# Mixer A: softmax denominators of eight key tiles by 128x32 products with ones in the four column groups of the array

## The chip, the cores and the metric

The kernel runs as one program on all 8 cores of one Trainium2 chip. Each core has its own TensorE (matrix products), VectorE, ScalarE, GpSimd, SyncE and DMA queues. Core c works on batch element c // 2 and on one half of its tokens as queries; cores don't exchange data. The metric is the time in microseconds of the slowest core. The profile pages and the rows below are of core 5, the slowest core of one profiled execution.

## The reference

One bidirectional encoder layer on x (4, 2048, 2048). What matters here is mixer A, a dense attention with 8 query heads and 2 key/value heads of width 128:

```python
h = rms_norm(x, norm_gain[l])
proj = jnp.einsum('bsd,dc->bsc', h, w_in[l])
...
qa = axial_rotary(rms_norm(qa.reshape(B, S, A_Q_HEADS, HEAD_DIM), q_norm_gain[l]), row_id, col_id)
ka = axial_rotary(rms_norm(ka.reshape(B, S, A_KV_HEADS, HEAD_DIM), k_norm_gain[l]), row_id, col_id)
ya = grid_gqa_attention(qa, ka, va) * jax.nn.silu(ga)       # (B, S, A_WIDTH)
```

with, inside the attention:

```python
s = jnp.einsum('bqhgd,bkhd->bhgqk', q_blk, k).astype(jnp.float32) * scale
p = jax.nn.softmax(s, axis=-1).astype(v.dtype)
return jnp.einsum('bhgqk,bkhd->bqhgd', p, v)
```

Mixer B (dilated windows in three groups), the merge of the two branches under sigmoid gates, the output projection with the residual and a final RMS norm follow.

## The kernel before

**Stages.** Each core first normalises its batch element's 2048 tokens into hT (2048 features by 2048 tokens, bfloat16). It then projects keys and values of mixer A, and after that runs two things interleaved on TensorE: the attention of mixer A, and the projections of mixer A's queries and gates and, as they finish, those of mixer B. Mixer B's attention comes next, again among projections, then the merge over 16 column tiles, then the output projection.

**One block of mixer A** is one head h and one half qb of the core's 1024 queries, 16 blocks in all. The 2048 keys are 16 tiles kc of 128. For each tile, attA_S makes the scores, transposed (128 keys by 512 queries), in one of three PSUM banks; ScalarE takes the exponential into one of eight buffers pbufs (0 to 3 in s_arena, 4 to 7 in s_gain), in bfloat16. No maximum is subtracted. attA_PV multiplies the tile with V and sums over the 16 tiles in bank 6.

**The denominators** are the column sums of P over all 2048 keys. A product with a 128x128 matrix of ones gives the sum over the 128 keys of a tile, in all 128 partitions at once. That is done directly for the tiles kc 3, 7, 11, 14 and 15, in bank 7. The other eleven tiles, DSET, are summed element by element on VectorE into acc (float32, in s_gain). Then acc is split into two bfloat16 parts, hiP (a cast) and loP (acc less hiP, a subtraction), and two more products with ones in bank 7 (in epi) add the sums of the two. ScalarE makes the reciprocal as exp(-ln), into rec, VectorE multiplies bank 6 with it (tmp) and then with the gate, into yaT.

**A P buffer** is free again when its product with ones was issued, or, for a tile of DSET, when both the V product and the add have read it (p_used counts to 2).

**Order of the work.** The program is written out ahead of time by a planner. Each of the generators (attA_S, attA_PV, attA_sum, epi, proj_all and others) yields after a small piece of work; Streams.run always emits the piece whose first operation could start soonest by the planner's own clock, less a small bonus of its stream. The clock (Sched.ready and Sched.cost) adds up a cost for every operation and 0.18 us for a result from another engine. Pools stand for banks and buffers: X.alloc takes an item or blocks the stream, X.free gives it back at that point of the program. The engines then run their own lists in that order, and wait on semaphores for each other.

**Banks.** While mixer A's attention runs, three banks (0, 1, 2) are the pool "pj" of the projections, three (3, 4, 5) the pool "S" of the scores, 6 is "Oa" and 7 is "La". A projection unit (16 products of 512 columns, in pieces of four) needs two free banks of pj and takes one; the sums of squares for the norm of q take one for a moment. Each block goes with two projection units, one of a query head and one of a gate head. pj_bonus keeps the projections at most a little ahead of the attention.

Bank 6 is held from the block's first V product until tmp has been made, so the next block's V products wait for the end of this one's denominators.

Of the kernel before, what the change touches and what calls it, by code (L numbers as in the profile page):

```python
# [8 lines left out]
BF16 = mybir.dt.bfloat16  # L9
AF = mybir.ActivationFunctionType  # L10
# [12 lines left out]
class Sched:  # L23
# [41 lines left out]
    def cost(self, eng, method, kw):  # L65
        out = kw["ap"] if "ap" in kw else kw["out"]
        n = 1
        for d in out.shape[1:]:
            n *= d
        if eng == "pe":  # L70
            return max(0.066, n / 2400.0 + 0.002)
        if eng == "act":
            return 0.17 + 0.00084 * n
        if eng == "dve":
            fast = "in0" in kw and kw["in0"].dtype == BF16 and out.dtype == BF16
            return 0.15 + n / (1920.0 if fast else 960.0)
        return 0.3 + n / 960.0
# [271 lines left out]
def build_nc(debug=False, stop_after=None):  # L349
# [24 lines left out]
    with es:  # L374
        es.enter_context(nc.allow_low_precision("bf16 matmul operands, fp32 accumulation"))

        def sb(name, shape, dt):
            return es.enter_context(nc.sbuf_tensor(name, shape, dt))
# [15 lines left out]
        one_t = sb("s_one_t", [128, 1], F32)  # L394
        stat = sb("s_stat", [128, 64], F32)
        ones_t = sb("s_ones", [128, 128], BF16)
        pb = [es.enter_context(nc.psum_tensor("pb%d" % i, [128, 512], F32)) for i in range(8)]
        S = Sched(nc, es)

# [12 lines left out]
        def PS(i):  # L412
            return ("ps", i)
# [12 lines left out]
        def MM(out, lhsT, rhs, start, stop, reads, writes, inc=None):  # L426
            S.op("pe", "matmul", dict(out=out, lhsT=lhsT, rhs=rhs, start=start, stop=stop), reads, writes,
                 inc=(stop if inc is None else inc))
# [4 lines left out]
        def ACT(out, in_, func, reads, writes, **kw):  # L433
            S.op("act", "activation", dict(out=out, in_=in_, func=func, **kw), reads, writes)
# [4 lines left out]
        def CP(out, in_, reads, writes, eng="dve"):  # L439
            S.op(eng, "tensor_copy", dict(out=out, in_=in_), reads, writes)  # L440
# [8 lines left out]
        def MEMSET(ap, val, writes, eng="pool"):  # L449
            S.op(eng, "memset", dict(ap=ap, constant=val), (), writes)  # L450
# [110 lines left out]
        MEMSET(ones_t[:], 1.0, ["ones"], eng="dve")  # L561
        MEMSET(eps_t[:], EPS, ["eps"], eng="dve")
        MEMSET(one_t[:], 1.0, ["one"], eng="dve")
        ACT(stat[:, 0:1], one_t[:], AF.Ln, ["one"], ["pre"])
        S.dma("pool", rsm[:], ropeA_d, "c_rsm", writes=["rsm"])
        S.dma("pool", gnt[:], gn_d, "c_gnt", writes=["gnt"])
# [89 lines left out]
        acc = gain[:, 1024:1536]  # L656
        hiP = gain[:, 1536:1792].bitcast(BF16)
        loP = gain[:, 1792:2048].bitcast(BF16)
        DSET = (0, 1, 2, 4, 5, 6, 8, 9, 10, 12, 13)
        rec = af(11776, 12288)  # L660
        tmp = af(12288, 12800)

# [230 lines left out]
            X.later(f)  # L893

        def attA_sum():
            for h in range(8):
                for qb in range(2):
                    yield from X.alloc("acc")
                    first = None
                    for kc in DSET:  # L900
                        yield from ge(("P", h, qb, kc), 1)
                        p = X.get(("P", h, qb, kc)) - 1
                        if first is None:
                            first = (p, kc)
                            continue
                        if first != 0:
                            TT(acc, pbufs[first[0]], pbufs[p], ALU.add, [("pbuf", first[0]), ("pbuf", p)], ["acc"])
                            p_used((h, qb, first[1]), first[0])
                            first = 0
                        else:  # L910
                            TT(acc, acc, pbufs[p], ALU.add, ["acc", ("pbuf", p)], ["acc"])
                        p_used((h, qb, kc), p)
                        yield
                    CP(hiP, acc, ["acc"], ["hiP"])
                    yield
                    TT(loP, acc, hiP, ALU.subtract, ["acc", "hiP"], ["loP"])
                    X.setf(("hl", h, qb))
                    yield

        def attA_PV():  # L920
            yield from ge("Oready", 1)
            for h in range(8):
                vtok = vatoks[h // 4]
                for qb in range(2):
                    yield from X.alloc("Oa")
                    pe_first = True
                    for kc in range(16):
                        yield from ge(("v", kc // 4, (kc // 2) % 2), 1)
                        yield from ge(("P", h, qb, kc), 1)
                        p = X.get(("P", h, qb, kc)) - 1  # L930
                        if kc not in DSET and pe_first:
                            yield from X.alloc("La")
                        MM(pb[6][:], vtok[:, kc * 128:(kc + 1) * 128], pbufs[p], (kc == 0), (kc == 15),
                           [("vatok", kc // 4, (kc // 2) % 2), ("pbuf", p)], [PS(6)], inc=(kc in DSET or kc == 15))
                        if kc not in DSET:
                            MM(pb[7][:], ones_bf, pbufs[p], pe_first, False, ["ones", ("pbuf", p)], [PS(7)], inc=True)
                            pe_first = False
                            X.free("pb", p)
                        else:
                            p_used((h, qb, kc), p)  # L940
                        X.later(partial(at_add, 1.0 / 32))
                        yield

                    def epi(h=h, qb=qb):
                        yield from X.alloc("ep")
                        yield from ge(("hl", h, qb), 1)
                        MM(pb[7][:], ones_bf, hiP, False, False, ["ones", "hiP"], [PS(7)], inc=True)
                        yield
                        MM(pb[7][:], ones_bf, loP, False, True, ["ones", "loP"], [PS(7)])
                        X.free("acc", 0)  # L950
                        yield
                        ACT(rec, pb[7][:], AF.Ln, [PS(7)], ["rec"])
                        X.free("La", 7)
                        yield
                        ACT(rec, rec, AF.Exp, ["rec"], ["rec"], scale=-1.0)
                        yield
                        TT(tmp, pb[6][:], rec, ALU.mult, [PS(6), "rec"], ["tmp"])
                        X.free("Oa", 6)
                        yield
                        yield from ge(("sg", h, qb), 1)  # L960
                        TT(yaT[:, h, qb * 512:(qb + 1) * 512], tmp, sgas[h % 2][:, qb * 512:(qb + 1) * 512], ALU.mult,
                           ["tmp", ("sga", h % 2, qb)], [("yaT", h)])
                        X.free("ep", 0)
                        X.bump("E_done")
                        yield
                    fork(epi(), 0.5, "epiA")
                    yield

# [626 lines left out]
```

How the kernel before makes its waits and increments, by code:

```python
            def body(engine, prog=prog):  # L239
                for fn, waits, inc in prog:
                    for (s, v) in waits:
                        engine.wait_ge(s, v)
                    if fn is not None:
                        ins = getattr(engine, fn[0])(**fn[1])
                        if inc is not None:
                            ins.then_inc(inc[0], inc[1])
```

## Time and profile before

| | |
|---|---|
| median of 3 runs | 1170.87 us (1170.75 to 1171.92) |
| profiled execution, its own time | 1173.17 us |
| span of its slowest core, from the first to the last instruction | 1171.5 us |
| spans of the 8 cores | 1163.4 to 1171.5 us |
| granted TensorE clock, mean of a core | 0.991 to 0.997 of full speed |
| busy: TensorE, VectorE, ScalarE | 1131.8 us (97%), 625.4 us (53%), 518.3 us (44%) |
| instructions of the span | 18014 |

The difference between the profiled execution's time and the span is what lies before the first and behind the last instruction. Almost all operations go through one helper, so that every row has line 244: rows are told apart by the names of the tensors (output <- inputs; pb is PSUM, numbers left out) and by their shapes (in a product, 128*128 is the part of the array that is used, and 128x512 the output). A product's busy time counts overlap once; products overlap, as each lasts longer than the time to the next start.

### The profile page before, as it was taken

What the parts mean: (1) busy time and instruction counts of PE and PEld (TensorE: products, weight loads), DVE (VectorE), ACT (ScalarE), POOL (GpSimd) and SP (SyncE); (2) the same over time, 40 slices, a digit from 0 to 9 for tenths busy, and PEclk for the clock granted to TensorE, in tenths of its full rate; (3) what the DMA queues carried; (4) which work ended last, traced back from release to release, by engine and by line L of the source; (5) the groups of instructions that cost most, each with busy time, mean ns of one, the idle gap of its engine ahead of it and who ended that gap; (6) DMA issues with size and microseconds to landing.
All of it is one profiled execution on the core that took longest, in us unless ns stands there. A gap on an engine that the chain in (4) does not pass through costs nothing.

```text
span 1171.5 us, 18014 instructions; the slowest of 8 cores (1163.4 to 1171.5 us)
## 1 busy us (share of the span) xinstructions
PE 1131.8 (97%) x6052; PEld 563.5 (48%) x6052; DVE 625.4 (53%) x980; ACT 518.3 (44%) x914; POOL 81.1 (7%) x166
## 2 busy tenths in 40 slices
PE   3799999999999999999999999999999999999996
PEld 1668444444444545554554454444444444444443
DVE  4779878888886655663655555521212122122155
ACT  4675688888886544543543544411111111111232
POOL 1000100000000000000000000011111111010000
PEclk9999999999999999999999999999999999999999
DMA  7982711222232423423432420155656645449533
GB/s 186 251 262 37 126 35 22 36 37 37 37 73 37 90 37 57 70 42 51 71 55 37 73 46 5 19 90 94 117 88 115 100 71 87 74 89 246 130 145 144
DMA packets 28761, 100.16 MB, mean 86 GB/s; under 512 B 3168, under 2 KB 7280, under 8 KB 25600
## 3 DMA queue, kind: packets, MB, share of 16 engines
q0 software_dynamic: 20400, 63.34, 32.8%
q1 hardware_dynamic: 8272, 35.67, 9.1%
q8 instruction: 51, 0.84, 0.3%
q14 instruction: 38, 0.31, 0.1%
HBM read 153.87 MB, written 8.39 MB: 139 GB/s over the span
## 4 chain that ended last, share of the span: by engine, by line
PE 91%; DMA 5%; DVE 1%; ACT 1%; issue 1%; ACTq 0%; DVEq 0%; POOLq 0%; SPq 0%
PE pb L244 91%; DMA s_wsl<-w_in 2%; DVE s_gain L244 1%; DMA s_ybT<-xt 1%; DMA s_hT<-xt 1%; DMA s_yaT<-xt 1%; DMA s_arena<-xt 1%; ACT s_arena L244 0%; DVE s_arena L244 0%; ACT s_gain L244 0%; DVE s_yaT L244 0%; ACT s_wsl L244 0%; ACT s_stat L244 0%; ACTq L1482 0%; DVEq L242 0%
## 5 line engine op out<-in xcount | busy, mean ns | idle before, releaser
L244 PE MATMUL pb<-s_hT,s_wsl 128*128 128x512 bf16 (+2 forms) x3584 | 749.3, 362 | 3.2 <-DVE s_hT L244 1.9
L244 PEld LDWEIGHTS pb<-s_hT,s_wsl 128*128 128x128 bf16 x3584 | 341.8, 98 | 361.0 <-issue 10.2
L244 ACT ACTIVATE s_arena<-pb 128x512 bf16<-128x512 f32 (+6 forms) x472 | 262.5, 573 | 248.6 <-PE pb L244 184.2
L244 DVE TENSOR_TENSOR s_arena<-pb,s_arena 128x512 f32<-128x512 f32 x112 | 89.2, 797 | 291.2 <-PE pb L244 284.9
L244 ACT ACTIVATE s_arena<-pb,s_mb 128x512 f32<-128x512 f32 x64 | 43.8, 687 | 246.2 <-PE pb L244 246.2
L244 PE MATMUL pb<-s_arena 128*128 128x512 bf16 (+3 forms) x704 | 138.2, 308 | 0.0
L244 DVE TENSOR_TENSOR s_arena<-s_arena 64x512 bf16<-64x512 f32 (+2 forms) x128 | 100.6, 786 | 19.8 <-ACT s_arena L244 12.5
L244 POOL DMA_DIRECT2D s_wsl<-w_in x92 | 48.9, 532 | 842.4 <-PE pb L244 762.2
L244 DVE TENSOR_TENSOR s_arena<-s_arena,s_rope 128x512 f32<-128x512 f32 (+3 forms) x136 | 89.8, 661 | 3.8
L244 PEld LDWEIGHTS pb<-s_arena 128*128 128x128 bf16 x704 | 60.1, 98 | 54.3 <-issue 2.8
L244 DVE TENSOR_TENSOR s_gain<-s_gain 128x512 f32<-128x512 f32 x96 | 66.3, 691 | 19.5 <-ACT s_gain L244 9.6
L244 ACT ACTIVATE s_gain<-pb 128x512 bf16<-128x512 f32 x128 | 69.6, 597 | 11.1 <-PE pb L244 9.9
L244 DVE TENSOR_TENSOR s_arena<-pb,s_rope 64x512 f32<-64x512 f32 (+1 forms) x64 | 40.7, 636 | 37.8 <-ACT s_arena L244 37.7
L244 PE MATMUL pb<-s_yaT,s_wsl 128*128 128x512 bf16 x256 | 57.9, 379 | 0.0
L244 PE MATMUL pb<-s_hT,s_arena 128*128 128x512 bf16 x256 | 55.4, 379 | 0.0
L244 ACT ACTIVATE s_arena<-s_arena 128x512 f32<-128x512 f32 x80 | 49.9, 631 | 11.5 <-DVE s_arena L244 7.8
L244 DVE TENSOR_TENSOR s_gain<-s_gain,s_arena 128x512 f32<-128x512 f32 x64 | 44.3, 692 | 10.6 <-DVE s_gain L244 9.5
L244 PE MATMUL pb<-s_gain,s_arena 128*128 128x512 bf16 x128 | 45.7, 383 | 0.1
L244 PE MATMUL pb<-s_wsl,s_ones 128*128 128x256 bf16 x128 | 18.5, 295 | 22.6 <-ACT s_wsl L244 22.6
L244 DVE COPY s_arena<-pb 128x1024 bf16<-128x1024 bf16 (+3 forms) x40 | 24.6, 615 | 29.0 <-PE pb L244 28.6
L244 PEld LDWEIGHTS pb<-s_yaT,s_wsl 128*128 128x128 bf16 x256 | 25.1, 98 | 30.2
L244 PEld LDWEIGHTS pb<-s_hT,s_arena 128*128 128x128 bf16 x256 | 25.0, 98 | 30.2
(77 smaller groups left out, 643.8 us busy)
## 6 DMA issues: line engine op xcount, KB each, us to landing
s_wsl<-w_in POOLq DMA_DIRECT2D x92, 512.0 KB, 5.1
y<-s_arena SPq DMA_DIRECT2D x14, 512.0 KB, 3.0
s_yaT<-xt SPq DMA_DIRECT2D x6, 1024.0 KB, 9.8
s_arena<-xt SPq DMA_DIRECT2D x4, 1024.0 KB, 17.3
s_wsl<-wba POOLq DMA_DIRECT2D x16, 256.0 KB, 4.0
s_hT<-xr SPq DMA_DIRECT2D x4, 1024.0 KB, 16.0
s_hT<-wout POOLq DMA_DIRECT2D x8, 512.0 KB, 33.4
s_ybT<-xt SPq DMA_DIRECT2D x2, 1024.0 KB, 16.1
```

The lines of the kernel that those rows point to most:

```text
L244: ins = getattr(engine, fn[0])(**fn[1])
```

## The change

Before, five tiles of a block go through full products with ones and eleven are summed on VectorE. After:

- VectorE sums seven tiles (0, 3, 6, 9, 12, 13, 14).
- Eight tiles form two quads, (1, 2, 4, 5) and (7, 8, 10, 11). When the V product of a quad's last tile has been issued, four products follow, one for each tile, with a 128x32 matrix whose elements are 1/32. The one of tile j of the quad writes the partitions 32j to 32j+31 of bank 7; the second quad adds to the first. Each partition of group j then holds 1/32 of the sum over the keys of two tiles.
- After tile 13, VectorE adds bank 7 to acc (float32) and bank 7 is given back. The later product with the full matrix of ones sums over all 128 partitions, so the 32 copies of 1/32 give the sum.
- Tile 15 keeps its full product with ones. It and the two of hiP and loP go to a bank taken from the pool pj, held from there until Ln has read it.
- The planner counts a product of 32 output partitions at 0.35 of the columns. attA_sum waits until banks 6 and 7 have left the projection's pool.

```diff
-            return max(0.066, n / 2400.0 + 0.002)
+            return max(0.066, n * (0.35 if out.shape[0] == 32 else 1.0) / 2400.0 + 0.002)
...
+        ones32_t = sb("s_ones32", [128, 32], BF16)
+        ones32 = ones32_t[:]
...
+        MEMSET(ones32_t[:], 1.0 / 32, ["ones32"], eng="dve")
...
-        DSET = (0, 1, 2, 4, 5, 6, 8, 9, 10, 12, 13)
+        DSET = (0, 3, 6, 9, 12, 13, 14)
+        QUADS = ((1, 2, 4, 5), (7, 8, 10, 11))
...
         def attA_sum():
+            yield from ge("Oready", 1)
...
                         p_used((h, qb, kc), p)
                         yield
+                        if kc == 13:
+                            yield from ge(("quad", h, qb), len(QUADS))
+                            TT(acc, acc, pb[7][:], ALU.add, ["acc", PS(7)], ["acc"])
+                            X.free("La", 7)
+                            yield
...
-                        if kc not in DSET and pe_first:
-                            yield from X.alloc("La")
+                        last = [r for r in QUADS if r[-1] == kc]
                         MM(pb[6][:], vtok[:, kc * 128:(kc + 1) * 128], pbufs[p], (kc == 0), (kc == 15),
                            [("vatok", kc // 4, (kc // 2) % 2), ("pbuf", p)], [PS(6)], inc=(kc in DSET or kc == 15))
-                        if kc not in DSET:
-                            MM(pb[7][:], ones_bf, pbufs[p], pe_first, False, ["ones", ("pbuf", p)], [PS(7)], inc=True)
-                            pe_first = False
+                        if kc in DSET:
+                            p_used((h, qb, kc), p)
+                        elif any(kc in r for r in QUADS):
+                            held[kc] = p
+                        else:
+                            yield
+                            new = lb is None
+                            if new:
+                                lb = yield from X.alloc("pj")
+                            MM(pb[lb][:], ones_bf, pbufs[p], new, False, ["ones", ("pbuf", p)], [PS(lb)], inc=True)
                             X.free("pb", p)
-                        else:
-                            p_used((h, qb, kc), p)
+                        if last:
+                            qi = QUADS.index(last[0])
+                            if qi == 0:
+                                yield from X.alloc("La")
+                            for j, k4 in enumerate(last[0]):
+                                MM(pb[7][32 * j:32 * j + 32, :], ones32, pbufs[held[k4]], (qi == 0), (qi == len(QUADS) - 1),
+                                   ["ones32", ("pbuf", held[k4])], [PS(7)], inc=(j == 3))
+                            for k4 in last[0]:
+                                X.free("pb", held[k4])
+                            X.bump(("quad", h, qb))
...
-                        MM(pb[7][:], ones_bf, hiP, False, False, ["ones", "hiP"], [PS(7)], inc=True)
+                        MM(pb[lb][:], ones_bf, hiP, new, False, ["ones", "hiP"], [PS(lb)], inc=True)
                         yield
-                        MM(pb[7][:], ones_bf, loP, False, True, ["ones", "loP"], [PS(7)])
+                        MM(pb[lb][:], ones_bf, loP, False, True, ["ones", "loP"], [PS(lb)])
                         X.free("acc", 0)
                         yield
-                        ACT(rec, pb[7][:], AF.Ln, [PS(7)], ["rec"])
-                        X.free("La", 7)
+                        ACT(rec, pb[lb][:], AF.Ln, [PS(lb)], ["rec"])
+                        X.free("pj", lb)
```

## Rows read from the trace of the kernel before

**Rows 1.** The page: span, busy times, and the chain that ended last.

```profile
span 1171.5 us, 18014 instructions; the slowest of 8 cores (1163.4 to 1171.5 us)
...
PE 1131.8 (97%) x6052; PEld 563.5 (48%) x6052; DVE 625.4 (53%) x980; ACT 518.3 (44%) x914; POOL 81.1 (7%) x166
...
PE 91%; DMA 5%; DVE 1%; ACT 1%; issue 1%; ACTq 0%; DVEq 0%; POOLq 0%; SPq 0%
```

**Rows 2.** Busy us and instructions of each engine in three stretches.

```profile
core 5: us, PE busy (x) PEld busy (x) DVE busy (x) ACT busy (x) POOL busy (x), PEclk, DMA share, GB/s
132.00:390.00 258.00, 255.37 (x1196) 113.89 (x1195) 206.14 (x316) 203.75 (x378) 10.26 (x22) 0.99 0.27 47
390.00:750.00 360.00, 359.70 (x2186) 187.12 (x2185) 206.67 (x308) 162.26 (x290) 20.06 (x45) 1.00 0.29 50
750.00:1000.00 250.00, 250.00 (x1160) 113.32 (x1159) 56.86 (x84) 39.90 (x58) 31.65 (x60) 1.00 0.56 93
```

**Rows 3.** The chain in order of time, 206 to 223 us: start, length, what.

```profile
206.89 0.11 issue
207.00 15.70 PE pb L244 x72
222.70 0.11 issue
```

**Rows 4.** The timeline at a block's end: start, length, engine, operation.

```profile
220.59 1.03 PE L244 MATMUL pb<-s_hT,s_wsl 128*128 128x512 bf16 x4
220.65 0.69 DVE L244 TENSOR_TENSOR s_gain<-s_gain 128x512 f32<-128x512 f32 x1 [0.17 <-ACT s_gain L244]
...
221.44 0.43 DVE L244 CAST s_gain<-s_gain 128x512 bf16<-128x512 f32 x1
...
221.97 0.69 DVE L244 TENSOR_TENSOR s_gain<-s_gain 128x512 bf16<-128x512 f32 x1
...
222.11 1.08 PE L244 MATMUL pb<-s_gain,s_ones 128*128 128x512 bf16 x3
...
223.28 0.60 ACT L244 ACTIVATE s_arena<-pb 128x512 f32<-128x512 f32 x1 [0.57 <-PE pb L244]
...
223.67 2.54 PE L244 MATMUL pb<-s_hT,s_wsl 128*128 128x512 bf16 x11
223.97 0.63 ACT L244 ACTIVATE s_arena<-s_arena 128x512 f32<-128x512 f32 x1
...
224.71 0.69 DVE L244 TENSOR_TENSOR s_arena<-pb,s_arena 128x512 f32<-128x512 f32 x1 [0.34 <-PE pb L244]
```

**Rows 5.** Groups by form: projections, products with ones; busy us, mean ns | idle before, releaser.

```profile
L244 PE MATMUL pb<-s_hT,s_wsl 128*128 128x512 bf16 x3072 | 695.1, 379 | 0.5 <-DMA s_wsl<-w_in 0.5
...
L244 PE MATMUL pb<-s_gain,s_ones 128*128 128x512 bf16 x80 | 27.4, 382 | 2.5 <-DVE s_gain L244 1.8
L244 PE MATMUL pb<-s_arena,s_ones 128*128 128x512 bf16 x64 | 24.2, 381 | 1.9 <-ACT s_arena L244 1.3 <-DVE s_arena L244 0.5
```

**Rows 6.** The timeline where short products stand among full ones, with weight loads.

```profile
457.68 0.40 PE L244 MATMUL pb<-s_arena 128*128 128x64 bf16 x8
457.91 1.46 PE L244 MATMUL pb<-s_hT,s_wsl 128*128 128x512 bf16 x6
...
457.46 0.49 PEld L244 LDWEIGHTS pb<-s_arena 128*128 128x128 bf16 x8
...
L244 PE MATMUL pb<-s_arena 128*128 128x64 bf16 x128 | 6.2, 193 | 0.0
```

**Rows 7.** Groups by form, VectorE: an add, and one that reads a bank.

```profile
L244 DVE TENSOR_TENSOR s_gain<-s_gain 128x512 f32<-128x512 f32 x80 | 55.3, 691 | 18.0 <-ACT s_gain L244 9.6 <-DVE s_gain L244 6.6 <-ACT s_arena L244 1.7
L244 DVE TENSOR_TENSOR s_arena<-s_arena,pb 128x512 f32<-128x512 f32 x24 | 16.4, 682 | 11.6 <-ACT s_arena L244 11.5
```

**Rows 8.** Groups by form: weight loads of the V products.

```profile
L244 PEld LDWEIGHTS pb<-s_gain,s_arena 128*128 128x128 bf16 x128 | 12.6, 98 | 16.2 <-issue 2.6
```

**Rows 9.** Instructions on the gain buffers: min/median/max ns, first and last start.

```profile
L244 DVE TENSOR_TENSOR s_gain<-s_arena x16: 682/684/693, 109.5 to 369.5; 128x512 f32<-128x512 bf16 x16
```

More of the change, by code:

```diff
@@ L925, in attA_PV @@
                     yield from X.alloc("Oa")
-                    pe_first = True
+                    lb = None
+                    held = {}
                     for kc in range(16):
@@ L941, in attA_PV, with epi @@
                         X.later(partial(at_add, 1.0 / 32))
                         yield
-                    def epi(h=h, qb=qb):
+                    def epi(h=h, qb=qb, lb=lb):
                         yield from X.alloc("ep")
                         yield from ge(("hl", h, qb), 1)
-                        MM(pb[7][:], ones_bf, hiP, False, False, ["ones", "hiP"], [PS(7)], inc=True)
+                        new = lb is None
+                        if new:
+                            lb = yield from X.alloc("pj")
+                        MM(pb[lb][:], ones_bf, hiP, new, False, ["ones", "hiP"], [PS(lb)], inc=True)
```

## The prediction

> **What bounds the kernel now.** I read the page's busy shares and its chain first, to see which engine sets the end. TensorE is busy for 97% of the span and 91% of the chain is matrix products [rows 1]. VectorE and ScalarE are busy half of the time, so their work counts only where TensorE stands waiting for it. Next come the busy times by stretch: mixer A's attention runs from about 132 to 390 us, and there TensorE is busy 255.4 of 258.0 us, VectorE 206.1 and ScalarE 203.8 [rows 2]. Behind it, from 390 to 750 us (mixer B) and on to 1000 us (merge), TensorE has no idle time worth the name [rows 2]. A column of matrix work removed in mixer A is thus not absorbed later: what follows is a fixed amount of TensorE work. And at most 2.6 us of idle time can be recovered there.
>
> The chain in time shows the rhythm: between two issue gaps of 0.11 us there are 72 products in 15.70 us, so one (h, qb) block lasts 15.81 us [rows 3]. The code gives the same 72: 16 score products, 16 products with V, 5 products with ones (kc 3, 7, 11, 14, 15), 2 for hiP and loP, 32 of two projection units, and one sum of squares. Eleven 512-column products of the projection that start in a row take 2.54 us, and one lasts 0.379 us [rows 4, 5], so products start (2.54 - 0.379) / 10 = 0.216 us apart, and 72 x 0.216 = 15.55 us. The remaining 0.26 us of the block is one wait: three products with ones take 1.08 us where 2 x 0.216 + 0.379 = 0.81 would do, since the last of them needs loP, which VectorE ends at 221.97 + 0.69 = 222.66 us [rows 4]. The group of products with ones on these buffers shows it as well: TensorE stood idle 2.5 us ahead of them, 1.8 of it for VectorE [rows 5].
>
> The whole gain must therefore come from TensorE columns in 16 blocks; the time that it takes from VectorE is worth something only at that loP wait.
>
> **What goes.** Per block four 128x512 products with ones leave (kc 3, 7, 11, 14; kc 15 keeps its full product): 4 x 0.216 = 0.864 us, times 16 blocks = 13.8 us. The row of products with ones on the gain buffers has 80, that on the arena buffers 64; together 144 = 16 x 7 + 24 sums of squares of q and k + 8 of mixer B, so 7 per block is the right count [rows 5]. All are in a stretch where TensorE never rests, so all of this is on the path.
>
> **What comes.** Per block eight products of 128x32 by 512 columns, in two groups of four, each group in the four column groups of one bank. The trace has no product with fewer than 128 columns of weights, so the cost of a group has to be bounded. Let a group cost one stream of 512 columns plus three staggers.
> - From below: no stagger, 0.216 us a group, 32 x 0.216 = 6.9 us, net -6.9 us.
> - From rows: eight products of 64 columns, each with a weight load of its own, take 0.40 us, one of them 0.193, so they start (0.40 - 0.193) / 7 = 0.030 us apart [rows 6]. That is the rate at which TensorE begins short products. A group is then 0.216 + 3 x 0.030 = 0.305 us, 32 groups 9.8 us, net -4.1 us.
> - The eight weight loads beside them take 0.49 us, so they start (0.49 - 0.098) / 7 = 0.056 us apart [rows 6]. If the stagger is that of the loads: 0.384 us a group, 12.3 us, net -1.5 us.
> - From above: the four do not overlap at all, 0.864 us a group, 27.6 us, net +13.8 us.
>
> I take 0.305 us. In the row a load is taken ahead while earlier products stream (the first of the eight loads starts at 457.46, its product at 457.68), and the narrow loads go to different column groups with a quarter of the columns each, so the begin rate of products, not that of loads, is the nearest row.
>
> The Trainium skill, on its page TensorE: Matmul & The Clock Gate, part 3 on packing small matmuls, states about 4 ns per further tile and that an output's start partition chooses the column group. By that a group would be 0.216 + 0.012 = 0.228 us and the net -6.5 us; no row here shows two products in the array side by side, and the sum above does not use it.
>
> **VectorE.** Before: 10 adds, a cast and a subtraction per block. After: 6 adds of P tiles and one of bank 7. An add is 0.691 us, and the nearest row for one that reads a bank is 0.682 us [rows 7]. Three fewer per block is 2.1 us, 33 us over 16 blocks, of 206 in the stage. Valued at nothing: TensorE covers it. If cover were gone, VectorE would be less of a bound than before, not more.
>
> **The end of a block.** Here the change adds a wait. Before, the last tile that VectorE adds is kc 13 (220.65), then comes the cast (221.44) and the subtraction (221.97), and kc 14 is a product [rows 4]. After, kc 13 is followed by the add of bank 7, by kc 14, and only then by the cast. Two adds of 0.69 us with 0.17 us ahead of each (as that of row 220.65) make hiP and loP 1.7 us later. Queued behind them: on TensorE the two products with ones, on ScalarE Ln and Exp of rec (223.28, 223.97), on VectorE the product that ends bank 6 (224.71 to 225.40) [rows 4]. So bank 6 comes free at about 227.1 instead of 225.4, and the next block's V products start that much later. What covers it is work that needs neither: the order holds eleven projection products in a row there [rows 4], another 1.7 us wants eight more, and the eight P buffers let scores run ahead. The written order is recomputed with these due times, so TensorE's instructions are placed for it. I cost it at nothing and keep the 0.26 us wait as it is. From above: the whole 1.7 us uncovered in each block, +27 us, which would need an order with nothing to put there; half a microsecond of it is what I take for the rival. From below: an order that also hides the present wait gains 2.6 us.
>
> The bank for the sums (lb) now comes from the projection's pool of three, from kc 15 until Ln. A new projection unit must leave one bank free. In the block shown the unit that fills the time starts at 220.59, ahead of kc 15, and ends at 226.2, while Ln has read its bank by 223.9 [rows 4], or 225.6 with the delay. The pool is thus free again when the next unit wants to start: nothing. If not, it is the same idle time as that of the late hiP, and the same rival.
>
> One more constant is written once at the start on VectorE, a quarter of the columns of the ones beside it, off the path. No DMA is added or moved. P tiles of a quad are held until its fourth tile: at most four of eight buffers, with three score banks behind them; nothing. The sums now start only once bank 7 is out of the projection's pool, so in the first block the early adds (the first at 109.5 us) move to where the attention's stretch begins, at about 132 us [rows 9]; VectorE is busy 80% of that stretch [rows 2], less with the change, and a block of 15.8 us holds seven adds of 0.69: nothing.
>
> **Sum.** -13.8 + 9.8 = -4.1 us on a profiled execution whose span is 1171.5 us and whose time is 1173.17. The median of the runs is 2.3 us below that, and as a difference carries over, 1170.87 - 4.1 = 1166.8 us (-0.35%).
>
> **Rivals.**
> 1. *The array empties at each change of shape* (slower). The row shows that a product lasts 0.379 us while the next starts after 0.216: 0.163 us of each lies under its successor [rows 4]. If a 128x32 product cannot start until the 128x128 one is out, and the reverse, each group pays this twice: 32 x 2 x 0.163 = +10.4 us, net +6.3 us, 1177.2. If the weight loads at both changes can't be taken ahead either, 64 x 0.098 = 6.3 more [rows 8]: 1183.5. It decides against the change once a group costs over 13.8 / 32 = 0.43 us, that is 0.13 us more than I take. For it: no row has two shapes of weights in turn, so nothing shows it is free. Against it: products of 512 columns, eight of 64 and again 512 follow each other with no gap (457.68 to 457.91 for the eight) [rows 6], though all with full weights. The Trainium skill's page TensorEngine Tiling (Array Packing), key properties, states that "changing tiling mode (not just tile) drains the TensorE", which is this rival; no row here shows it.
> 2. *Half of that*: only the way in or the way out costs 0.163 us: +5.2 us, net +1.1 us, 1172.0, no change that can be told.
> 3. *The four don't overlap*: +13.8 us, 1184.7. The change would then not do what it says. For it only that no row shows overlap.
> 4. *The late hiP*: 0.5 us idle in each block, +8 us, net +4 us, 1174.9. Against it the cover counted above.
> 5. *The order also hides the present wait*: -2.6 us more, 1164.2.
>
> **Chances.** The overlap with a stagger between 0 and 0.056 us: 0.52 (most of it near -4, some 0.04 within 0.2%). Rival 1: 0.14. Rival 2: 0.12. Rival 3: 0.08. Rival 4: 0.10. Rival 5: 0.04. A measurement of this kernel tells 0.2%, 2.3 us, from no change. Faster by more than that: 0.48 + 0.04 = 0.52. Within: 0.12 + 0.04 = 0.16. Slower: 0.32. The likeliest case alone runs from 1164.0 to 1169.4 us. The range from 1163.0 to 1179.0 us takes in rivals 2, 4 and 5 and the lower half of rival 1; outside are rival 3, the upper half of rival 1 and a little below: 0.17.
>
> **What would show it.** The starts of the four 128x32 products of a group, 0.03 us apart if I am right, 0.216 apart in rival 3. The time from the last full product ahead of a group to its first narrow one, and from its fourth to the next full one: 0.216 each if nothing empties, 0.38 or more in rival 1. The period of a block: 15.81 - 4.1 / 16 = 15.55 us. VectorE's busy time between 132 and 390 us down by some 33 us. TensorE's waits on VectorE for the gain buffers: about as now, many times more in rival 4. The prediction is wrong if a group costs over 0.38 us, or if idle time of TensorE in the stage grows by over 2 us.

## The result, and the profile after

The changed kernel takes 1176.5 us (median of 6 runs, 1175.07 to 1241.24) against 1170.91 before (6 runs): a ratio of 1.0045, 95% interval 1.0034 to 1.0057. By that ratio it is 5.3 us slower; 1166.8 us was predicted, in a range of 1163.0 to 1179.0. Runs in which one die was disturbed, such as the one of 1241 us, count in the medians here and below but are left out of the ratios.

The page of the changed kernel is of core 4. First its busy times, then the chain by engine, which answer to [rows 1]:

```profile
PE 1126.0 (96%) x6003; PEld 559.0 (48%) x6116; DVE 592.7 (50%) x933; ACT 521.4 (44%) x914; POOL 81.5 (7%) x166
...
PE 82%; DVE 8%; DMA 4%; issue 3%; ACT 3%; DVEq 0%; ACTq 0%; SPq 0%; POOLq 0%
```

VectorE has 33 us less to do and yet its share of the chain rose from 1% to 8%. That is the first thing to see: less busy, and more in the way. (Core 5 shows 8% as well. The share is only a hint: in e3 below it is 4%, with a block just as long.) On this core 113 records of products are missing (6003 of 6116), so from here on core 5 is read, where none is. Its busy times by stretch, columns as in [rows 2]:

```profile
132.00:390.00 258.00, 253.18 (x1252) 107.55 (x1251) 173.27 (x267) 204.54 (x375) 10.78 (x23) 1.00 0.27 46
390.00:750.00 360.00, 359.56 (x2184) 186.78 (x2183) 205.79 (x308) 162.60 (x291) 20.02 (x45) 1.00 0.29 50
```

In mixer A's attention TensorE is idle for 4.8 us where it was 2.6; behind it little changed (0.44 us idle from 390 to 750 us, 0.30 before). VectorE is down from 206 to 173 us there. The attention itself is longer. VectorE writes yaT once a block; the first and last of these 16 writes on core 1, before and after (min/median/max ns, first and last start):

```profile
L244 DVE TENSOR_TENSOR s_yaT<-s_arena x16: 692/692/693, 142.2 to 387.6; 128x512 bf16<-128x512 f32 x16
```

```profile
L244 DVE TENSOR_TENSOR s_yaT<-s_arena x16: 691/693/693, 141.6 to 392.8; 128x512 bf16<-128x512 f32 x16
```

That is 245.4 us before and 251.2 after, 5.8 us more. Of that, the first twelve intervals between these writes hold 1.7 us and the last three 4.1; the last blocks hold a varying share of mixer B's projections, so this alone is rough. What TensorE waited for between 132 and 400 us on that core (us in total, times, longest), after; before there was one such row, 1.8 us in 5 waits for VectorE's s_gain:

```profile
PE pb L244 <- DVE s_gain L244: 3.2, 14, 0.3
PE pb L244 <- DVE s_arena L244: 1.9, 1, 1.9
PE pb L244 <- ACT s_gain L244: 0.8, 1, 0.8
PE pb L244 <- ACT s_arena L244: 0.2, 1, 0.2
```

The 14 waits are those for loP. The three below are single ones that the new order brought, near the start and the end of the attention: at 155.25 and 156.46 us for exponentials, and at 353.52 us for VectorE.

The counts of this view mislead in one point. A late product shows as idle time only as far as the one ahead no longer covers it, and a shorter delay gets no releaser: the 0.26 us of every block before stands in [rows 3] as an "issue" of 0.11. So I also add up, from the starts, by how much each product begins later than 0.216 us after the one ahead (from 128 to 420 us, delays of 0.06 us and more). The products with hiP and loP are late by 4.5 us in all before and by 6.6 us after, on every core with a full record. All others together are late by 0.3 to 0.7 us before and by 2.6 to 4.0 after, which is mostly the three single waits.

**The groups.** The timeline of core 5 around one quad, with weight loads:

```profile
240.92 0.59 PE L244 MATMUL pb<-s_gain,s_arena 128*128 128x512 bf16 x2
241.45 0.09 PEld L244 LDWEIGHTS pb<-s_gain,s_ones 128*32 128x32 bf16 x1 [0.42 <-issue]
241.45 0.39 PE L244 MATMUL pb<-s_gain,s_ones 128*32 128x512 bf16 x1
...
241.45 0.39 PE L244 MATMUL pb<-s_arena,s_ones 128*32 128x512 bf16 x1
...
241.45 0.39 PE L244 MATMUL pb<-s_gain,s_ones 128*32 128x512 bf16 x2
...
241.78 0.11 PEld L244 LDWEIGHTS pb<-s_arena 128*128 128x128 bf16 x2 [0.23 <-issue]
241.78 0.39 PE L244 MATMUL pb<-s_arena 128*128 128x512 bf16 x1
```

The four narrow products start together, within 0.01 us. But the last full product ahead started at 240.92 + 0.216 = 241.14, so the group begins 0.31 us after it instead of 0.216, and the next full product begins 0.33 us after the group instead of 0.216. A group costs 0.31 + 0.33 - 0.216 = 0.43 us, rounded up. In the starts to the nanosecond all 32 groups on this core cost 0.422 to 0.426 us, 13.6 us together.

**The block.** The chain in order of time, from one block's Ln for the norm of q (224.71) to the next one's (240.75). Pieces shorter than 0.1 us are left out:

```profile
224.71 0.70 ACT s_arena L244
...
225.49 0.64 ACT s_arena L244
...
226.22 0.76 DVE s_arena L244
...
227.08 0.69 DVE s_arena L244
...
227.80 0.69 DVE s_arena L244
...
228.52 0.70 DVE s_arena L244
...
229.37 0.55 issue
229.92 0.70 DVE s_gain L244
...
230.78 0.70 DVE s_gain L244
...
231.64 0.70 DVE s_gain L244
...
232.50 0.70 DVE s_gain L244
...
233.37 0.70 DVE s_gain L244
...
234.23 0.70 DVE s_gain L244
...
235.02 0.44 DVE s_gain L244
...
235.56 0.70 DVE s_gain L244
236.26 0.14 issue
236.39 4.28 PE pb L244 x19
...
240.75 0.70 ACT s_arena L244
```

This is a ring. Ln and Exp of the norm of q (ScalarE, on the sum of squares of the projection unit), the norm and the rope products of q (VectorE, s_arena), then six dependent adds to acc, the cast and the subtraction (s_gain), then TensorE's product with loP at 236.39 and 18 products behind it, the last of them the sum of squares of the next unit, and Ln again. One turn takes 240.75 - 224.71 = 16.04 us. It is not held by a buffer: each arrow is either a true dependence or the fixed order of an engine's list. The six adds (five of P tiles, one of bank 7) take 0.86 us each: 0.69 and 0.17 of waiting for the one ahead.

Before, 15.70 of 15.81 us of a block were products in a row [rows 3], but VectorE's list shows that it held the pace there too. The kernel before, core 5, from tmp on:

```profile
208.89 0.69 DVE L244 TENSOR_TENSOR s_arena<-pb,s_arena 128x512 f32<-128x512 f32 x1 [0.34 <-PE pb L244]
209.69 0.69 DVE L244 TENSOR_TENSOR s_yaT<-s_arena 128x512 bf16<-128x512 f32 x1
...
212.53 0.68 DVE L244 TENSOR_TENSOR s_gain<-s_arena 128x512 f32<-128x512 bf16 x1
```

Then follow the other nine adds, the last at 220.65, the cast and loP, which ends at 222.66, and in all this VectorE never stands for more than 0.18 us. Behind it come loP's product, Ln (223.28) and Exp (223.97) of rec and the next tmp at 224.71 [rows 4]: 15.82 us after 208.89. The 0.26 us over TensorE's 15.55 were thus a ring through VectorE already, by another way. This is read from the timeline and was not tried by itself; e12 fits it.

TensorE's own work in a block is now 68 full products and two groups, 68 x 0.216 + 2 x 0.43 = 15.5 us, what it was (72 x 0.216). So the change saves nothing on TensorE, and the ring makes this block 16.04 us where it was 15.81. Not all 16 blocks are like this one: over all of them the waits for hiP and loP grow by 2.1 us (4.5 to 6.6). The three single waits, 2.9 us idle on core 1 and 1.5 on core 5, come on top.

### The profile page after: what moved, and what is told of

It is laid out like the page before. It is cut to its first block, busy times and chain, and to the rows that moved or that the text cites. A ratio compares the mean times of both kernels' runs of the same rounds, so it can differ in the third digit from the quotient of the medians.

```text
span 1175.6 us, 17765 instructions; the slowest of 8 cores (1168.3 to 1175.6 us)
## 1 busy us (share of the span) xinstructions
PE 1126.0 (96%) x6003; PEld 559.0 (48%) x6116; DVE 592.7 (50%) x933; ACT 521.4 (44%) x914; POOL 81.5 (7%) x166
## 4 chain that ended last, share of the span: by engine, by line
PE 82%; DVE 8%; DMA 4%; issue 3%; ACT 3%; DVEq 0%; ACTq 0%; SPq 0%; POOLq 0%
PE pb L244 82%; DVE s_gain L244 4%; DMA s_yaT<-xt 3%; DVE s_arena L244 2%; ACT s_arena L244 2%; DVE s_hT L244 1%; DMA s_gain<-xt 1%; DMA s_wsl<-w_in 1%; ACT s_wsl L244 0%; DVEq L242 0%; ACT s_gain L244 0%; DVE s_yaT L244 0%; ACT s_rs L244 0%; ACT s_stat L244 0%; ACTq L242 0%
## 5 line engine op out<-in xcount | busy, mean ns | idle before, releaser
L244 ACT ACTIVATE s_arena<-pb 128x512 bf16<-128x512 f32 (+7 forms) x473 | 264.2, 574 | 236.1 <-PE pb L244 177.4
L244 PE MATMUL pb<-s_arena 128*128 128x512 bf16 (+3 forms) x697 | 142.1, 306 | 2.8 <-DVE s_arena L244 1.4
L244 ACT ACTIVATE s_gain<-pb 128x512 bf16<-128x512 f32 x127 | 73.2, 598 | 18.2 <-PE pb L244 17.6
L244 DVE TENSOR_TENSOR s_gain<-s_gain 128x512 f32<-128x512 f32 (+1 forms) x83 | 57.4, 691 | 22.6 <-ACT s_gain L244 14.0
L244 PE MATMUL pb<-s_gain,s_arena 128*128 128x512 bf16 x123 | 43.2, 380 | 0.0
L244 PE MATMUL pb<-s_arena,s_ones 128*32 128x512 bf16 (+2 forms) x180 | 39.6, 346 | 3.0 <-ACT s_arena L244 2.4
## 6 DMA issues: line engine op xcount, KB each, us to landing
s_ybT<-xt SPq DMA_DIRECT2D x2, 1024.0 KB, 15.5
```

The costliest lines, as they stand in the source:

```text
L244: ins = getattr(engine, fn[0])(**fn[1])
```

## The experiments

Ratios are to the kernel before, with their intervals. Twelve kernels ran. In e1, e2, e5, e6 and e9 the lists of instructions are edited after the planner is done, so that every engine keeps the changed kernel's order; the others are written out anew. In the diffs a line that begins with # says what the lines left out do.

**e1: one full product in place of each group.**

```diff
+ # four narrow products of a quad -> one full product on its last tile
+ kw = dict(grp[3][0][1], out=pb[7][:], lhsT=ones_bf)
+ new.append((("matmul", kw), [w for g in grp for w in g[1]], grp[3][2]))
```

> Each group of four 128x32 products is replaced by one full 128x512 product with ones on the quad's last tile (three tiles are left out of the sum); all else, the order of every engine included, is that of the changed kernel. Theory 1 (a group costs 0.43 us on the path, 0.21 more than its 512 columns, as the spacing of starts in the changed kernel's trace shows): 32 x (0.43 - 0.216) = 6.8 us less than the changed kernel, about 1169.5 us, ratio to before 0.999. Theory 2 (the loss is all in the waits for hiP and loP at the block's end, and what a group costs is hidden there): at most 2 us less, 1174.5 us.

Measured: 1174.44 us, 1.0028 (1.0017 to 1.0038): 2 us less than the changed kernel, not 6.8. The timeline of TensorE at the end of a block (core 5):

```profile
233.50 0.38 PE L244 MATMUL pb<-s_arena,s_ones 128*128 128x512 bf16 x1
234.29 0.38 PE L244 MATMUL pb<-s_gain,s_ones 128*128 128x512 bf16 x1 [0.41 <-DVE s_gain L244]
234.50 0.38 PE L244 MATMUL pb<-s_arena 128*128 128x512 bf16 x1
235.09 0.38 PE L244 MATMUL pb<-s_gain,s_ones 128*128 128x512 bf16 x1 [0.21 <-DVE s_gain L244]
```

The products with hiP and loP start 0.79 and 0.59 us after the one ahead, 0.94 us in all more than twice 0.216. In the changed kernel the same two waits add up to 0.49 us (235.25 to 235.60 and 235.81 to 236.39). The 0.43 us a block that the groups gave back became waiting for VectorE; the yaT writes stay 16.05 us apart (221.73, 237.78). Of the two theories the second holds: something that doesn't pass through the groups sets the block.

**e2: each group doubled.**

```diff
+ # the four narrow products, and the same four once more
+ new += [(("matmul", dict(g[0][1], stop=False)), g[1], None) for g in grp]
+ new += [(("matmul", dict(g[0][1], start=False)), [], g[2]) for g in grp]
```

> Each group of four narrow products is issued twice in a row, eight narrow products together, so eight tiles count twice in the denominators; the order is otherwise that of the changed kernel. Theory 1a (the extra 0.21 us is paid at the change between full and narrow products, once for each group): 32 x 0.216 = 6.9 us more than the changed kernel, about 1183 us. Theory 1b (four narrow products side by side take 0.43 us in themselves): 13.7 us more, 1190 us. No overlap at all would give 27.6 us more.

Measured: 1178.16 us, 1.006 (1.0047 to 1.0073), 2 us more than the changed kernel. The total is smaller than either theory said, for the reason of e1: 0.43 us a block went into the wait that was there. What a group costs is read in the timeline instead (core 5):

```profile
229.11 0.81 PE L244 MATMUL pb<-s_arena 128*128 128x512 bf16 x3
229.85 0.39 PE L244 MATMUL pb<-s_arena,s_ones 128*32 128x512 bf16 x1
...
230.08 0.38 PE L244 MATMUL pb<-s_gain,s_ones 128*32 128x512 bf16 x1
...
230.40 0.39 PE L244 MATMUL pb<-s_gain,s_arena 128*128 128x512 bf16 x1
```

The second four start 0.23 us after the first of the first four, 0.216 after the last of them, like full products; only the way in (229.54 to 229.85) and the way out (230.08 to 230.40) have their extra 0.1 us. That is theory 1a, the surcharge is paid at the change of shape.

**e3: bank 7 added one tile earlier.**

```diff
-                        if kc == 13:
+                        if kc == 12:
```

> VectorE adds bank 7 to acc after tile 12, not after tile 13; the same operations. hiP and loP then follow the last exponentials by one add less (0.69 us and 0.17 us ahead of it). If the doubled wait at the block's end (0.58 us a block, 0.26 before) comes from the longer chain on VectorE: 2 to 5 us less than the changed kernel, 1171.5 to 1174.5 us. If it comes from the bank that is now taken from the projections' pool: no change, 1176 us.

Measured: 1178.21 us, 1.0059 (1.0046 to 1.0073), no gain. As I had put it that spoke for the bank from the projections' pool, but the expectation was wrong in itself: in a ring of dependent adds it doesn't matter in which order they stand. The yaT writes stay 16.04 us apart.

**e4: the planner's clock knows VectorE's gap.**

```diff
-            t = max(t, k[4] + (0.0 if k[2] == eng else 0.18))
+            t = max(t, k[4] + ((0.12 if eng == "dve" else 0.0) if k[2] == eng else 0.18))
```

> The same operations as the changed kernel, written out in another order: the planner's clock now adds 0.12 us where a VectorE operation follows one that it depends on (the trace shows 0.17 us idle there). If the waits for hiP and loP come from a plan that believes them ready too soon: the waits shrink and the kernel is 3 to 5 us faster than the changed one, 1171.5 to 1173.5 us. If the buffers and banks leave nothing to put there, no change, 1176 us.

Measured: 1177.21 us, 1.0049 (1.0035 to 1.0063), no gain. The waits for hiP and loP are gone from the view of waits, but the new order has others: on core 5, 3.5 us in 5 waits for VectorE's s_arena and 0.5 us in one for ScalarE, and a block of 15.97 us.

After these four I had the ring of the changed kernel's chain as the theory, and took one piece out of it.

**e5: one add of the ring made short, all orders kept.**

```diff
+ # the last add to acc before the cast, 8 of its 512 columns
+ kw = {k: (v if k == "op" else v[:, 0:8]) for k, v in kw.items()}
+ dve[last_add] = ((m, kw), w, inc)
```

> The changed kernel, every engine in its order, but VectorE's last add of a block (tile 14 to acc) covers 8 of 512 columns, so tile 14 is left out of nearly all sums; that add takes some 0.06 us in place of 0.69. Loop theory: the 16.04 us of a block are a ring through the engines' fixed orders (loP's product, 19 products, sum of squares of q, Ln, Exp, the rope operations on VectorE, the adds, the cast, the subtraction, loP's product again), which shrinks by 0.63 us to 15.41; TensorE's own work of 68 full products and two groups, 15.5 us, then takes over: a block of about 15.55 us, 5 to 8 us less than the changed kernel, 1169 to 1171.5 us. If TensorE's columns set the block already, or the bank taken from the projections' pool does: no change, 1176 us.

Measured: 1170.67 us, 0.9994 (0.9984 to 1.0004), 6 us less than the changed kernel. VectorE's writes of yaT in two blocks (core 5):

```profile
219.76 0.69 DVE L244 TENSOR_TENSOR s_yaT<-s_arena 128x512 bf16<-128x512 f32 x1
235.31 0.69 DVE L244 TENSOR_TENSOR s_yaT<-s_arena 128x512 bf16<-128x512 f32 x1
```

15.55 us apart: TensorE's 15.5 us and no wait. The waits for VectorE's s_gain fell from 3.2 us in 14 to 0.3 in 2 on core 1, and the three single waits are still there, no smaller, which is why it is not 4 us below the kernel before. Counted from the starts, the delay of the hiP and loP products falls from 6.6 to 0.7 us, the 6 us measured. The banks and TensorE's list were untouched, so the bank taken from the projections does not hold this order back. One thing was not as expected: the short add took 0.17 us and not 0.06, so the ring shrank by 0.52 us, to 15.52, and hardly lies under TensorE's work. VectorE's work ahead of loP is shown to set the block of the changed kernel; that it closes to a ring is settled by the next run.

**e6: the short add and the full products together.** The edits of e5 and e1.

> The last run's short add (tile 14 left out of nearly all sums) together with one full product in place of each group of four narrow ones (three tiles of a quad left out), all orders kept. With full products alone the block stayed at 16.04 us. Loop theory: ring 15.41 us, TensorE's work 70 x 0.216 = 15.1 us, so the block is 15.4 us, 2 to 3 us less than with the short add alone and 9 to 10 us less than the changed kernel: about 1167 us. If a group costs nothing on the path: the same as the short add alone.

Measured: 1168.8 us, 0.9978 (0.9969 to 0.9987), 2 us less than e5. The yaT writes are at 217.80 and 233.32, 15.52 us apart in this block; with 15.1 us of work on TensorE, the shortened ring is again what is left: 16.04 - 0.52 = 15.52, less by just what the short add gives back. The chain view of this run names an exponential ahead of the short add (228.32 to 228.92, the add at 228.99). That is a coincidence in time: in the changed kernel the same add starts at 234.23 and the same exponential ends at 234.60, so the add can't be waiting for it, and in both it starts 0.86 us after the add ahead.

**e7 and e8: other shares of the work.**

```diff
# e7
-        DSET = (0, 3, 6, 9, 12, 13, 14)
-        QUADS = ((1, 2, 4, 5), (7, 8, 10, 11))
+        DSET = (0, 1, 2, 4, 5, 6, 8, 9, 12, 13)
+        QUADS = ((3, 7, 10, 11),)
...
-                        if kc == 13:
+                        if kc == 12:
# e8
-        DSET = (0, 3, 6, 9, 12, 13, 14)
+        DSET = (0, 3, 6, 9, 12, 13)
...
-                        if kc == 13:
+                        if kc == 12:
```

> All sums complete: one quad (3, 7, 10, 11), VectorE adds ten tiles (0, 1, 2, 4, 5, 6, 8, 9, 12, 13) and bank 7 after tile 12, tiles 14 and 15 have full products. TensorE has 69 full products and one group a block: 69 x 0.216 + 0.43 = 15.33 us against 15.55 before; VectorE has ten adds as before. Theory (what counts is the sum on TensorE as long as VectorE's ring is not longer): 15.33 us plus the wait of before, 0.26: 3.5 us less than before, 1167.5 us. If the ring through VectorE takes over: above 1171 us.

> All sums complete: two quads as in the changed kernel, but tile 14 has a full product and VectorE adds six tiles and bank 7 (after tile 13). The ring is shorter by one add (0.86 us with the gap ahead of it), TensorE's work is 69 full products and two groups, 15.74 us. Loop theory: a block of 15.75 to 15.9 us, 3 to 4 us less than the changed kernel, about 1172.5 us. If the bank or the groups were the cause: not less than 1176 us, rather 3.5 us more for the extra product.

Measured: e7 1183.02 us, 1.0102 (1.0088 to 1.0117); e8 1179.61 us, 1.0071 (1.0057 to 1.0086). Both missed. (In e8 bank 7 was in fact added after tile 12, not 13 as the expectation says.) e7 has the least work on TensorE of all complete versions and is the second slowest. The timelines of TensorE, e7 and then e8 (core 5):

```profile
235.13 0.38 PE L244 MATMUL pb<-s_arena,s_ones 128*128 128x512 bf16 x1 [0.19 <-ACT s_arena L244]
236.33 0.90 PE L244 MATMUL pb<-s_arena 128*128 128x512 bf16 x3 [0.83 <-ACT s_arena L244]
```

```profile
242.62 0.38 PE L244 MATMUL pb<-s_gain,s_arena 128*128 128x512 bf16 x1 [0.67 <-DVE s_arena L244]
```

In e7 TensorE waits for ScalarE, in e8 for tmp, which frees bank 6. Each share gives an order with a wait of its own, so these two say nothing against the ring of the changed kernel's order, and nothing for the prices that they were meant to weigh.

**e9: two groups of two instead of one of four.**

```diff
+ # the last V product moves between the second and third narrow one
+ new = new[:-1] + grp[:2] + [new[-1]] + grp[2:]
```

> All sums complete, the changed kernel's orders, but the last V product ahead of each quad now stands between its second and third narrow product, so every quad is two groups of two. If what a group costs beyond its 512 columns (0.21 us) is paid at each change between full and narrow products, a group of two also costs 0.43 us, TensorE's work is 68 x 0.216 + 4 x 0.43 = 16.4 us a block, above the ring of 16.04 us, and the kernel is some 5 us slower than the changed one, 1181 us. If the cost goes with the number of narrow products: no change, 1176 us.

Measured: 1183.36 us, 1.0104 (1.009 to 1.0118), 7 us more than the changed kernel, for the same products. The timeline (core 5):

```profile
225.11 0.38 PE L244 MATMUL pb<-s_gain,s_arena 128*128 128x512 bf16 x1
225.42 0.39 PE L244 MATMUL pb<-s_arena,s_ones 128*32 128x512 bf16 x2
225.75 0.39 PE L244 MATMUL pb<-s_gain,s_arena 128*128 128x512 bf16 x1
226.07 0.39 PE L244 MATMUL pb<-s_gain,s_ones 128*32 128x512 bf16 x2
226.39 0.82 PE L244 MATMUL pb<-s_arena 128*128 128x512 bf16 x3
```

0.31, 0.33, 0.32 and 0.32 us from start to start: every change of shape costs 0.1 us over 0.216, in either direction, for two narrow products as for four. The yaT writes are 16.39 us apart (223.55, 239.94), the 16.4 that was worked out. The products with hiP and loP are late by 1.0 us in all, where it was 6.6: with more work of its own, TensorE no longer waits for the ring.

**e10: the planner with both measured prices.** The edit of e4, and in the planner's cost:

```diff
-            return max(0.066, n * (0.35 if out.shape[0] == 32 else 1.0) / 2400.0 + 0.002)
+            return max(0.066, n * (0.5 if out.shape[0] == 32 else 1.0) / 2400.0 + 0.002)
```

> The changed kernel's operations, written out by a planner whose clock has both measured prices: 0.12 us where a VectorE operation follows one that it depends on, and 0.5 of the columns for a narrow product (0.43 us a group). If the loss comes from orders planned with wrong prices: a block near TensorE's own 15.5 us plus a small wait, 1169 to 1172 us. If the greedy order is a matter of chance, anything from 1168 to 1183 us, as the orders so far gave.

Measured: 1178.84 us, 1.0068 (1.0055 to 1.008). Both prices right gave no better order.

**e11: the adds ahead of the rope operations.**

```diff
-        X.spawn(attA_sum(), 0.2, "sumA")
+        X.spawn(attA_sum(), 0.6, "sumA")
```

> The changed kernel, with the bonus of the stream of adds raised from 0.2 to 0.6, above that of the rope operations (0.3). In the ring the rope operations of q stand ahead of six adds on VectorE. If the adds go first, the ring loses the 2 to 4 us of rope operations and TensorE's 15.5 us set the block: 1168 to 1171 us. If the adds are not ready earlier, no change, 1176 us.

Measured: 1171.56 us, 1.0003 (0.9994 to 1.0011), 5 us less than the changed kernel with the same operations, all sums complete. The chain from 224 to 242 us (core 5) is one piece:

```profile
223.99 18.15 PE pb L244 x90
```

VectorE's list now has adds between the rope operations of q, and the hiP and loP products are late by 2.6 us in all, less than the 4.5 of the kernel before; the other delays, 2.8 to 3.1 us, make up for it. With the ring broken up, TensorE sets the time in this stretch again, and the change is worth nothing: it removed 13.8 us of products, and its groups cost 13.6.

**e12: the kernel before with the planner's clock of e4.** The same edit on the kernel before.

> The kernel before, only with the planner's clock adding 0.12 us where a VectorE operation follows one that it depends on. It tells how much a rewritten order alone moves the time. If the wait of 0.26 us for loP goes: 4 us faster, 1167 us; if it is chance, up to 1% either way.

Measured: 1172.01 us, 1.0009 (1.0 to 1.0018), no change that counts. Its chain from 200 to 260 us has no wait left either (first line below), but from 390 to 750 us TensorE is idle 2.2 us where it was 0.3 (second line, columns as in [rows 2]):

```profile
200.00 60.01 PE pb L244 x278
```

```profile
390.00:750.00 360.00, 357.80 (x2146) 184.16 (x2145) 204.04 (x302) 159.71 (x284) 19.51 (x44) 1.00 0.30 47
```

So the 0.26 us for loP can be had by another order, with the same work on VectorE (a block is 15.54 us), and here it was given back by other waits, 1.9 us of them in mixer B.

## Why the prediction was wrong

*What goes* held as a count: four full products a block, 13.8 us. TensorE is the bound when nothing else is late (e11).

*What comes* was mis-sized, and it is the largest part of the miss. The term was 0.305 us a group from three staggers of 0.03. Measured, the four start within 0.01 us of each other, and instead there is 0.09 us on the way in and 0.11 on the way out: 0.43 us a group, 13.6 us in place of 9.8. That is 3.8 us, nearly the whole forecast gain. The step that failed is the choice of the row. I read the 0.030 us between products of 64 columns as the rate at which TensorE begins short products. In the trace of the kernel before (core 5) products of 512, 256, 128 and 64 columns follow each other after 0.216, 0.109, 0.056 and 0.029 us (medians): so 0.030 is what 64 columns take, and it says nothing of how four products side by side begin. No row showed a change of shape. The break-even that the prediction named under rival 1, 0.43 us, is where it fell. That rival had the right place and kind (e2, e9) but over half again the price: I had put 0.163 us on each change, the part of a product that lies under its successor; it is 0.10. In size alone rival 2 was nearer. The Trainium skill's rule that changing the tiling mode drains TensorE (TensorEngine Tiling (Array Packing), key properties) agrees in kind with these starts, 0.09 and 0.11 us later than between full products. The 4 ns per further tile that the Trainium skill states (TensorE: Matmul & The Clock Gate, part 3) agrees with a group's starts, 0.009 to 0.011 us over three steps. The narrow weight loads start together with their products, and so does the first full load after a group, while before a full product they run one product ahead. Whether the 0.1 us is the load that isn't taken ahead (0.098 us by [rows 8]) or the array that empties, these runs don't tell apart.

*VectorE, valued at nothing,* and *the end of a block, costed at nothing,* are the second step that failed; with the single waits it turns no gain into a loss. I looked for cover behind hiP and loP, found enough products, and TensorE indeed never waits long there: 0.49 us a block. But I asked only what is late behind the adds, not what stands ahead of them in VectorE's list. The written order put the rope operations of q ahead of six dependent adds, and these ahead of loP, and loP ahead of the next sum of squares. That closed a ring of 16.04 us, longer than TensorE's 15.5. Moving three adds off VectorE did not shorten it. I had also not seen that the 0.26 us before was such a ring, and not one late operation; and the "at most 2.6 us" to be recovered counts idle time only, where 16 blocks of 0.26 are 4.2 us. Rival 4 named the place, but 0.5 us a block on top of the 0.26, where it is 0.49 in all, and its reason was a longer end without cover, not work ahead of the adds. My "if cover were gone, VectorE would be less of a bound than before" was wrong outright: VectorE went from 1% to 8% of the chain with 33 us less work.

*The written order, taken to place the work for it,* is the third. It brought single waits for exponentials and for VectorE that no rival had.

The sum as measured, against the kernel before: from the groups, 13.6 - 13.8 = -0.2 us; from the hiP and loP products, 6.6 - 4.5 = 2.1 us; from all other delays, 1.8 to 3.3 us by core, most of it the single waits. Together 3.7 to 5.2, and 5.3 was found. Both signs that the prediction had set for being wrong are there: a group costs over 0.38 us, and TensorE's idle time in the stage grew by 2.2 us. Removing nearly all waits of the ring gave 6 us back (e5), which is more than the ring had added, since the kernel before paid 4.5 us of it too; another order of the same operations gave 5 (e11). The single waits were read from the trace and not taken out by an experiment of their own. The bank for the sums, rightly costed at nothing for this order, may still have shaped it when it was planned; that was not tried by itself.

## What to carry to other kernels

Packing narrow products into column groups pays only for runs of them: here a change of shape costs 0.1 us each way, so four products of 512 columns in one group cost as much as two full ones, and eight in a row as much as three (e2). When a list is written out in advance, an engine with a third of its time free can still set the pace through a ring of true dependences and list order; look at the period of the loop and walk the chain once around before calling its work free, also where the page shows the matrix engine in one unbroken piece. And an edit that makes a greedy planner write a new order brings that order's waits with it, up to 1% here: judge the edit with orders kept, and the order apart.

## What was not expected of the hardware

- Four 128x32 products in the four column groups start within 0.01 us of each other and stream side by side; eight in a row take two slots of 0.22 us.
- Every change between a 128x128 and a 128x32 product adds 0.09 to 0.11 us to the 0.216 between starts, in both directions, for two, four or eight narrow products.
- VectorE adds that depend on each other start 0.86 us apart, 0.17 more than their 0.69 us; rope operations with no wait between them, 0.72 us apart (227.08, 227.80, 228.52).
